# Which PSUM bank each half of the next pair's projections uses while forgetting attention runs

## The reference, cut to what matters

```python
def mixer_sb_fox(x, w_in, b_f, w_o):
    h = x @ w_in
    ...
    oa = stick_breaking_attention(qa, ka, va).reshape(b, s, -1)
    ob = forgetting_attention(qb, kb, vb, f_logit).reshape(b, s, -1)
    return jnp.concatenate([oa, ob], axis=-1) @ w_o

def forgetting_attention(q, k, v, f_logit):
    cum = jnp.cumsum(jax.nn.log_sigmoid(f_logit.astype(F32)), axis=1)
    ...
        logits = (jnp.einsum('bqhd,bshd->bhqs', qb.astype(F32), kf) * scale
                  + cq.transpose(0, 2, 1)[..., None] - cum_k[:, :, None, :])
        p = jax.nn.softmax(jnp.where(mask, logits, -jnp.inf), axis=-1)
        return jnp.einsum('bhqs,bshd->bqhd', p, vf)
```

## Time and profile before

| | us |
|---|---|
| median of 3 runs | 2824.18 |
| lowest and highest | 2823.06, 2825.07 |
| the profiled execution | 2827.21 |
| its span | 2825.4 |

### The profile page before, as it was taken

How to read it: one execution, slowest core, us unless ns; L and a number is a source line. 1 busy time by engine, 2 the same in 40 slices (tenths; PEclk the granted TensorE clock), 3 DMA queues, 4 the chain that set the end, 5 groups by cost and what they waited for, 6 DMA issues and landing times.

```text
span 2825.4 us, 42474 instructions
## 1 busy us (share of the span) xinstructions
PE 2687.5 (95%) x15813; PEld 1363.5 (48%) x16096; DVE 1903.7 (67%) x2637; ACT 1080.0 (38%) x1665; POOL 1676.1 (59%) x916
## 2 busy tenths in 40 slices
PE   7999898899999999999899999899999999999998
PEld 4666554354444444444444444456654444444443
DVE  6788778575666674256999999688847656664043
ACT  3566566243333210014554343666643433331000
POOL 4777656336676679845347777711113666675884
PEclk9999999999999999999999999999999999999999
DMA  4122455631111253332213222488873111113332
GB/s 150 50 64 72 90 119 119 193 115 60 58 53 55 68 179 127 105 132 83 53 38 142 111 79 100 114 183 185 185 208 132 68 60 60 60 54 126 127 105 97
DMA packets 299309, 294.82 MB, mean 104 GB/s; under 512 B 239408, under 2 KB 239536, under 8 KB 299168
## 3 DMA queue, kind: packets, MB, share of 16 engines
q1 hardware_dynamic: 287360, 268.90, 33.1%
q10 hardware_dynamic: 11808, 23.99, 2.6%
HBM read 189.51 MB, written 35.70 MB: 80 GB/s over the span
## 4 chain that ended last, share of the span: by engine, by line
PE 78%; DVE 6%; issue 5%; ACT 4%; DMA 4%; POOL 2%; ACTq 1%; POOLq 0%; DVEq 0%; SPq 0%
PE ps L1691 23%; PE ps L334 20%; PE ps L316 14%; PE ps L650 4%; PE ps L2529 4%; PE ps L399 4%; DMA pt<-split 3%; PE ps L920 2%; PE ps L2019 2%; PE ps L656 1%; PE ps L2063 1%; DVE split L848 1%; PE ps L2557 1%; PE ps L891 1%; DVE prob L1035 1%
## 5 line engine op out<-in xcount | busy, mean ns | idle before, releaser
L273 POOL TENSOR_TENSOR w_hi<-w_stage,ones 128x1024 bf16<-128x1024 f32 (+1 forms) x115 | 238.5, 2074 | 138.1 <-PE ps L334 85.3
L276 POOL TENSOR_TENSOR w_lo<-w_stage,w_hi 128x1024 bf16<-128x1024 f32 (+1 forms) x115 | 265.2, 2306 | 9.0
L1508 DVE SCALAR_TENSOR_TENSOR x_res<-x_res,ps 128x1024 f32<-128x1024 f32 x32 | 39.0, 1218 | 319.6 <-PE ps L334 318.8
L334 PE MATMUL ps<-w_hi,hid_hi 128*128 128x512 bf16 x689 | 206.4, 379 | 1.6 <-POOL w_lo L276 0.8
L334 PE MATMUL ps<-w_hi,hid_lo 128*128 128x512 bf16 x690 | 206.5, 379 | 0.7
L334 PE MATMUL ps<-w_lo,hid_hi 128*128 128x512 bf16 x690 | 206.4, 379 | 0.7
L2529 PE MATMUL ps<-lat_hi,q_now 128*128 128x512 bf16 (+3 forms) x736 | 185.9, 326 | 7.6 <-DVE row_max L2616 6.8
L316 PE MATMUL ps<-xt_hi,w_hi 128*128 128x512 bf16 x598 | 179.2, 380 | 3.1 <-DVE score L2178 2.5
L316 PE MATMUL ps<-xt_hi,w_lo 128*128 128x512 bf16 x596 | 179.0, 380 | 0.8 <-issue 0.2
L316 PE MATMUL ps<-xt_lo,w_hi 128*128 128x512 bf16 x592 | 178.1, 380 | 0.8
L1691 PE MATMUL ps<-xt_lo,w_hi 128*128 128x512 bf16 x426 | 161.5, 379 | 0.5
(11 more groups left out here) (309 smaller groups left out, 7507.6 us busy)
## 6 DMA issues: line engine op xcount, KB each, us to landing
w_stage<-in_l_up SPq DMA_DIRECT2D x88, 512.0 KB, 3.8
w_stage<-in_l_down SPq DMA_DIRECT2D x88, 512.0 KB, 3.7
w_stage<-in_l_o SPq DMA_DIRECT2D x32, 512.0 KB, 6.2
w_stage<-in_l_q SPq DMA_DIRECT2D x32, 512.0 KB, 5.1
q_split<-q_out SPq DMA_DIRECT2D x32, 512.0 KB, 2.6
q_now<-q_split SPq DMA_DIRECT2D x16, 1024.0 KB, 5.7
w_stage<-in_l_qkv SPq DMA_DIRECT2D x24, 512.0 KB, 4.1
x_spilled<-x_res ACTq DMA_DIRECT2D x16, 512.0 KB, 2.6
```

The costliest lines, as they stand in the source:

```text
L273: pool.tensor_tensor(hi, w_stage[slot][:, 0:cols], ones[:, 0:1].to_broadcast([P, cols]), ALU.mult).then_inc(w_cast[slot], 1)
L276: pool.tensor_tensor(lo, w_stage[slot][:, 0:cols], hi, ALU.subtract).then_inc(w_split[slot], 1)
L334: mm = pe.matmul(ps[:, bank + h, :], a[:, k, rows], w[:, h * HALF:(h + 1) * HALF], start=(k == first and m == 0), stop=(k == tiles - 1 and ...
```

## The change

While a forgetting pair runs, bank 5 is not needed for turning weights, since the DMA does that. The change lets the halves e = 0, 2 and 4 go to bank 5 there, and leaves e = 1, 3 and 5 in bank 4. The first matmul of a half then waits for the evacuation of half e-2 in place of e-1. Pair 4 follows a stick-breaking pair whose last weights are still turned through bank 5 in its first slots: there e=0 stays in bank 4, e=1 still waits for e=0, and e=2 waits until that turning is through (`turning.lo`). The evacuations read from the new bank. Stick-breaking pairs keep bank 4 for all.

```diff
-        def proj_bank(e, pair):
-
-            return 2 + e if isinstance(pair, int) and pair == 0 else 4
+        def proj_bank(e, pair, kind=None, prev=None):
+
+            if isinstance(pair, int) and pair == 0:
+                return 2 + e
+            return 5 if kind == "fox" and e % 2 == 0 and (prev == "fox" or e > 0) else 4
...
                     if isinstance(pair, int) and pair == 1 and e == 0:
                         pe.wait_ge(s_pjl, 3)
+                    elif kind == "fox" and prev == "sb" and e == 2:
+                        pe.wait_ge(turning.lo, BATCHES * FIRST_FOX)
+                    elif kind == "fox" and (prev == "fox" or e > 2):
+                        pe.wait_ge(s_pjl, 6 * pair + e - 1)
                     elif not first:
                         pe.wait_ge(s_pjl, 6 * pair + e)
...
-                return hi[:, cols], lo[:, cols], ps[:, proj_bank(e, pair), :]
+                return hi[:, cols], lo[:, cols], ps[:, proj_bank(e, pair, kind, prev), :]
```

More of the change, by code:

```diff
@@ L628, in program, with proj_half @@
         half_slots = [(0, 1), (2, 3, 4), (5, 6, 7), (8, 9), (10, 11, 12), (13, 14, 15)]
-        def proj_bank(e, pair):
-            return 2 + e if isinstance(pair, int) and pair == 0 else 4
-        def proj_half(pe, e, pair, units):
-            n, bank = e // 2, proj_bank(e, pair)
+        def proj_bank(e, pair, kind=None, prev=None):
+            if isinstance(pair, int) and pair == 0:
+                return 2 + e
+            return 5 if kind == "fox" and e % 2 == 0 and (prev == "fox" or e > 0) else 4
+        def proj_half(pe, e, pair, units, kind=None, prev=None):
+            n, bank = e // 2, proj_bank(e, pair, kind, prev)
             first = isinstance(pair, int) and pair == 0
@@ L664, in opens_half, with proj_slot @@
             return any(slots[0] == slot for slots in half_slots)
-        def proj_slot(pe, slot, pair):
+        def proj_slot(pe, slot, pair, kind, prev):
             for e, slots in enumerate(half_slots):
@@ L669, in proj_slot @@
                     at, of = slots.index(slot), len(slots)
-                    proj_half(pe, e, pair, range((8 * at + of - 1) // of, (8 * at + 8 + of - 1) // of))
+                    proj_half(pe, e, pair, range((8 * at + of - 1) // of, (8 * at + 8 + of - 1) // of), kind, prev)
         def proj_ends(slot, pair, project, first):
@@ L676, in proj_ends, with proj_dst @@
             return [(e, pair + 1) for e, slots in enumerate(half_slots) if project and slots[-1] + 1 == slot]
-        def proj_dst(e, pair):
+        def proj_dst(e, pair, kind, prev):
             if e < 4:
@@ L682, in proj_dst, with proj_evac_hi @@
                 cols = slice(e % 2 * HALF, (e % 2 + 1) * HALF)
-                return hi[:, cols], lo[:, cols], ps[:, proj_bank(e, pair), :]
+                return hi[:, cols], lo[:, cols], ps[:, proj_bank(e, pair, kind, prev), :]
             hv = e - 4
             return (nv_hi[:, 4 * hv:4 * hv + 4, :], nv_lo[:, 4 * hv:4 * hv + 4, :],
-                    ps[:, proj_bank(e, pair), :].rearrange("p (b n) -> p b n", b=4))
-        def proj_evac_hi(act, e, pair):
-            hi, _, src = proj_dst(e, pair)
+                    ps[:, proj_bank(e, pair, kind, prev), :].rearrange("p (b n) -> p b n", b=4))
+        def proj_evac_hi(act, e, pair, kind=None, prev=None):
+            hi, _, src = proj_dst(e, pair, kind, prev)
             act.wait_ge(s_pj, 6 * pair + e + 1)
@@ L696, in proj_evac_hi, with proj_evac_lo @@
             act.activation(hi, src, ACT.Copy).then_inc(s_pjh, 1)
-        def proj_evac_lo(dve, e, pair):
-            hi, lo, src = proj_dst(e, pair)
+        def proj_evac_lo(dve, e, pair, kind=None, prev=None):
+            hi, lo, src = proj_dst(e, pair, kind, prev)
             dve.wait_ge(s_pjh, 6 * pair + e + 1)
@@ L896, in pair_tensor @@
                     if project and not opens_half(slot):
-                        proj_slot(pe, slot, pair + 1)
+                        proj_slot(pe, slot, pair + 1, kind, prev)
                     if not project:
@@ L946, in pair_scalar @@
                 for e, p in proj_ends(slot, pair, project, prev is None) if kind else ():
-                    proj_evac_hi(act, e, p)
+                    proj_evac_hi(act, e, p, kind, prev)
                 turned, p, at = trailing(pair, slot, kind, prev, None, 1)
@@ L998, in pair_vector @@
                 for e, p in proj_ends(slot, pair, project, prev is None) if kind else ():
-                    proj_evac_lo(dve, e, p)
+                    proj_evac_lo(dve, e, p, kind, prev)
                 if kind == "fox":
```

## The result

| | before | changed |
|---|---|---|
| median, us | 2825.12 (17 runs) | 2830.59 (17 runs) |
| lowest and highest | 2823.06, 2827.43 | 2827.92, 2835.47 |
| mean granted clock in one series of runs that had both | 0.9921 | 0.9903 |

The ratio is 1.0018, 95% interval 1.0012 to 1.0024. So the changed kernel is slower by 3.4 to 6.8 us. The size is just under the 0.2% named in the prediction, but the sign is certain, and the time lies 1.3 us above the top of my range (0.9 us of that is the kernel before, whose median is 2825.12 in these 17 runs and was 2824.18 in the first 3). I use both.

A forecast was written before the change was run, and what follows sets the result against it. DVE, ACT and the transposing DMA were taken to pace the stretches holding the waits, PE the rest. Openings gained nothing through slot 8, 0.1 us through slot 0, clock cost 0: 2824.18 - 0.1 = 2824.1 us, range 2820.0 to 2829.3.

The forecast's parts named there:

- What bounds the kernel: Forgetting pairs: PE sets the pace in slots 8 to 10 and 0 to 2, DVE and ACT elsewhere, where the seven waits lie.
- The openings: Slots 5 and 13: six waits, 8.39 us together, go altogether; the 2.24 us in slot 2 of pair 4 stays.
- Rival C: Slots 5 and 13: a hidden dependence keeps six waits at the openings; same time, 2824.2; chance within the forecast's 0.63.
- Slot 5 to 8: Value products of slot 8 start as before, released by mix_lo or the DMA; PE's lead joins the wait; gain 0.
- rival A: Openings of slots 5 and 13 are worth their waits: full -8.4 us (2815.8) or half (2820); chance 0.08.
- Slot 13 to 0: Value products of slot 0 wait for the DMA or mix_lo, waits 1.5 to 1.8 us; gain taken as 0.1 us.
- DVE does gain: Slot 14's row maximum loses its 0.74 us wait for PE; this reaches slot 15's mix_lo, useless where the DMA is last.
- rival D: Slots 14 and 15: DVE's 0.74 us shift meets GpSimd's work otherwise; -1.5 to +1.5 us, 2822.7 to 2825.7; chance 0.13.
- A cost that the trace does not show: Slot 8: one joined 2.5 us wait may halve TensorE's clock; bounds 0 and +5.1 us, 0 taken.
- Rival B: Clock falls at slot 8 in three places: 1.7 us for one (2825.8), 5.1 for all (2829.2), up to 2834.3; chance 0.16.
- the threefold single form: Slot 8: one low-clock stretch of 3.4 us at each of three places, 5.1 us in all, 2829.2.
- the doubled form: Slot 8: each low-clock stretch followed by a second one, twice the cost, up to 2834.3; slower by over 0.2%, chance 0.04.

The follow-up runs named there:

- e4: The changed kernel, but half e=2 (slot 5) waits for e=1 as before, so only slot 13's openings are early: 2825.08 us, beside 2825.94 before.
- e3: The changed kernel, but half e=5 (slot 13) waits for e=4 as before, so only slot 5's openings are early: 2829.05 us, beside 2825.94 before.
- e13: The changed kernel with 4 unread matmuls at the start of PE's program: 2829.72 us, beside 2825.76 for the kernel before.
- e11: The kernel before with 4 unread matmuls at the start of PE's program: 2826.02 us, beside 2826.50 without them.
- e10: The changed kernel with 44 unread matmuls at the start of PE's program: 2834.78 us, beside 2825.61 for the kernel before.
- e9: The kernel before with 44 unread matmuls at the start of PE's program: 2830.35 us, beside 2825.61 without them.
- e1: The changed kernel's alternating banks, but each half still waits for the evacuation of the half before it: 2826.35 us, beside 2825.99 before.
- e12: The kernel before with 88 unread matmuls of 8 columns at the start of PE's program: 2828.28 us, beside 2826.50 without them.
- e14: The kernel before with 57 unread matmuls at the start of PE's program: 2830.01 us, beside 2825.76 without them.
- e2: The changed kernel with unread matmuls filling PE's waits ahead of the value products of slots 8 and 0: 2830.74 us, beside 2825.99 before.

## Why the prediction was wrong, point by point

*What bounds the kernel: right.* That PE's waits lie in a stretch paced by DVE, ACT and the transposing DMA was the main reading, and it held.

*The openings: right.* Six waits gone, the first one left (2.26 beside 2.24 us). Rival C is out.

*Slot 5 to 8: right in place and size, but for the clock.* Predicted were 0.6 us before the scores and 2.5 before the products; measured 0.67 to 0.68, and 2.39, 2.47, 2.48. The next product started 0.06 us after mix_lo or with the DMA, as before. From slot 8 of pair 4 to slot 8 of pair 5, with no low stretch between, it was 53.89 us (53.73 before); from pair 5 to pair 6 it was 59.09 (53.83 before), with three low stretches, where 53.8 had been forecast. Nothing was gained from the lead in any trace: rival A is out.

*Slot 13 to 0: a gain forecast, a loss measured.* I expected waits of 1.5 to 1.8 us, and they were 1.89, 3.00 and 2.06. The row maximum of slot 14 indeed no longer waited for PE, but it bought nothing: the split behind it took 1.62 us where before one took 1.20, and ended 3.71 us after the start of the split before it in either trace. The next split, of slot 15, took 1.07 us and not 0.70. These rows are DVE's, pair 5, the splits of before first and then the changed kernel:

```profile
400.32 1.20 DVE L848 SCALAR_TENSOR_TENSOR split<-take,row_inv,split 128x512 bf16<-128x512 f32 x1
...
402.93 0.70 DVE L848 SCALAR_TENSOR_TENSOR split<-take,row_inv,split 128x384 bf16<-128x384 f32 x1 [0.37 <-ACT split L843]
```

```profile
402.12 1.17 DVE L854 SCALAR_TENSOR_TENSOR split<-take,row_inv,split 128x640 bf16<-128x640 f32 x1
...
403.29 0.40 DVE L1008 TENSOR_REDUCE row_max<-ps 128x1 f32<-128x256 f32 x1
...
404.21 1.62 DVE L854 SCALAR_TENSOR_TENSOR split<-take,row_inv,split 128x512 bf16<-128x512 f32 x1 [0.34 <-ACT split L849]
...
407.24 1.07 DVE L854 SCALAR_TENSOR_TENSOR split<-take,row_inv,split 128x384 bf16<-128x384 f32 x1 [0.37 <-ACT split L849]
```

So the step "DVE does gain: ... that goes. It reaches the mix_lo of slot 15" failed: mix_lo came 0.37 us later behind the split of slot 13 and not earlier. In pair 6, where mix_lo is last, this is paid in full: from slot 12 to slot 0 it took 10.19 us in the changed kernel and in e4, and 9.82 in before and in e3, whose slot 13 is not early. My 0.1 us of gain should have been a loss of 0.4 there. Why the two splits take longer when they come earlier isn't shown.

The 3.00 us in pair 5 come from the queue of SP, which I had called unmoved. It shows the transposes of slots 12 to 15 of pair 5 and the weight loads between them; first the kernel before, then the changed one (start, duration):

```profile
393.70 5.00 SPq L856 DMA_TRANSPOSE turned<-split  x2
398.74 0.58 SPq L248 DMA_DIRECT2D w_stage<-in_l_o  x1
399.37 5.50 SPq L856 DMA_TRANSPOSE turned<-split  x3
```

```profile
398.01 5.18 SPq L862 DMA_TRANSPOSE turned<-split  x2
403.24 1.58 SPq L248 DMA_DIRECT2D w_stage<-in_l_o  x1
404.86 5.09 SPq L862 DMA_TRANSPOSE turned<-split  x3
```

The load held the queue for 1.58 us and not 0.58, the transpose behind it came 1 us later, and with it the products. In the second trace of the changed kernel it was 1.20; with the padding, without any lead of PE, the two transposes or one of them took longer instead, and the stretch from slot 12 to 0 was 11.29 us there and 11.14 here, beside 10.03 in before. Without any lead of PE that stretch lies between 10.03 and 12.02 us (the longest with the 88 matmuls), and with slot 13 alone early it was 10.10. So this microsecond is a meeting of the sort of rival D, and no work of the change alone. What lengthens the queue is open.

*"A cost that the trace does not show ... I take 0 for the likeliest": this step failed.* The mechanism, the place, the wait of 2.5 us and the price of 1.7 us for each stretch were all written down. The term was sized 0 and should have been about 5. I had two rows to go by, 2.25 us with a full clock behind it and 2.53 with a low one, said that 2.5 was nearer to the second, and then put 0 with the argument of dense work before it. The runs say that in this range a wait decides nothing by itself: 2.39 and 2.48 us went either way, and so did 2.06 (low behind it in the first trace) and 2.05 (full in the second). So the likeliest value for three places, each of which may fall singly, doubly or not at all, was one between the bounds, and neither bound. Two more things made it too small: I priced slot 8 only, though the waits of slot 0 came to 1.9 us and over too, and they were followed by low stretches in pairs 6 and 7; and I gave the doubled stretch to the far tail, while one of three falls at slot 8 in e3, and one of two in the changed kernel's first trace, were double. Rival B, with a chance of 0.16, is what happened.

How the loss divides can be read on the way, in the four traces of the changed kernel with and without padding. It is 7.5 and 4.8 us longer than before in the first two, and 5.5 and 6.4 longer than in the equally padded kernel before (e13 beside e11, e10 beside e9). Of these, 5.8, 3.4, 4.4 and 5.8 us stand right behind the value products with a low clock: a single low stretch at slot 8 made 7.3 us into 9.0 (the 1.7 forecast), a double one into 10.0 to 10.2 (2.7 to 2.9, and not twice 1.7), one at slot 0 of pair 6 cost 1.4 to 1.6. The rest, 0.6 to 1.6 us, stands between slots 12 and 0. The clock of all runs fits: 0.9903 beside 0.9921 is 0.0018 x 2826 = 5.1 us if PE is the bound wherever it falls, beside 4.8 in the median. Slot 5's openings bring 3.1 us, slot 13's -0.9 alone; with 2.5 us either way on each, their sum of 2.2 can't be told from the 4.8. The Trainium skill, page "TensorE: Matmul & The Clock Gate", section "HAM oscillation — how this bites in real kernels", tells of this kind of loss, in an example that waits for about 3 to 5 us each time. The traces agree, with 2 to 4 low stretches where before had none, but behind waits of only 2.05 to 3.03 us.

*The range.* Its top, 2829.3, was the threefold single form. The true time lies between that and the doubled form, 2834.3, which I had left out. The range was also called 8 in 10, while the chances that I put into it come to 0.92 (0.63, 0.13, 0.12 and 0.04). The 2830.59 lies above the 2829.8 that stood for slower by over 0.2%, but against the kernel before as measured beside it the ratio is 1.0018.

## What to carry to other kernels

A wait that is taken from an engine inside a stretch that others pace does not vanish: it joins the next wait of the same engine. Here waits of 1.5 and 1.65 us, with a full TensorE clock behind them in every trace of the kernel before, padded or not, became one of 2.4 to 2.5 us with a low clock behind it in 10 of 15 places, and the loss then fell on the stretch where TensorE is the bound. The freed buffer is worth something only if it lets real work of the bounded stretch move into that wait; here a reordering of one share of matmuls turned +4.8 us into -12.2.

## What the runs showed of the hardware beyond that

- The same wait before the same work (2.39, 2.48, 2.05 to 2.06 us) was followed by a granted clock of 0.50 in one execution or pair and of 1.00 in another. Each low stretch lasted 3.4 us or a multiple. At slot 8, where PE was the bound, a single one cost 1.7 us and a double one 2.7 to 2.9.
- Matmuls added in a wait at the start of PE's program, and never read, moved the time by -0.5 (4), +4.7 (44), +4.2 (57) and +1.8 us (88), each with about 2.5 us either way. In this kernel, a gain or loss under 5 us by an edit that adds instructions means little without a control with as many instructions and no edit.
- The same split of 384 columns on DVE took 0.67 to 0.71 us in slot 15 of pairs 4 to 6 wherever slot 13 waits as before (before, e1, e3, e9, e11, e12, e14), and 1.06 to 1.07 us wherever PE is early there (the changed kernel twice, e2, e4, e10, e13).
- One weight load held SP's queue for 0.58 to 1.58 us in the same place of the program, and what stood behind it came as much later.
